# A two-layer hybrid decoder trunk: first x fetched already transposed, products by parts at the layer joins, smaller masks

## The reference, cut to what matters

```
for l in range(2):
    h = h + mixer_sublayer(h, ...)      # below
    h = h + ffn_sublayer(h, ...)        # rms_norm; silu(h@w_gate)*(h@w_up); @w_down; rms_norm

# mixer_sublayer
z = rms_norm(x, norm_pre) @ w_in        # c_q 384 | c_kv 256 | k_r 32 | conv 2*512 | pool 512 | gates 3*1024
y_attn = attention, 8 heads, causal, from rms_norm(c_q) @ w_uq, rms_norm(c_kv) @ w_uk, @ w_uv
y_conv = silu(layer_norm(conv31(a * sigmoid(g)))) @ w_conv_o
y_pool = (pooled differences @ pool_w per group of 128 * pool_scale) @ w_pool_o
out = rms_norm((g0*y_attn + g1*y_conv + g2*y_pool) @ w_mix_o, norm_post)
```

## Time and profile before

| | |
|---|---|
| median of three runs | 823.91 us (823.85 to 823.97) |
| profiled execution, its own time | 823.19 us |
| its span | 821.4 us |
| TensorE matmul busy | 801.1 us, 98% of the span |
| VectorE busy | 554.3 us, 67% |
| ScalarE busy | 428.5 us, 52% |
| GpSimd busy | 92.4 us, 11% |
| DMA | 144.44 MB, mean 176 GB/s |

### The profile page before, as it was taken

How to read it: one execution, slowest core, us unless ns; L and a number is a source line. 1 busy time by engine, 2 the same in 40 slices (tenths; PEclk the granted TensorE clock), 3 DMA queues, 4 the chain that set the end, 5 groups by cost and what they waited for, 6 DMA issues and landing times.

```text
span 821.4 us, 10272 instructions
## 1 busy us (share of the span) xinstructions
PE 801.1 (98%) x3924; PEld 675.4 (82%) x3924; DVE 554.3 (67%) x770; ACT 428.5 (52%) x607; POOL 92.4 (11%) x112
## 2 busy tenths in 40 slices
PE   5999999999999999999999999999999999999996
PEld 4898888878878888988879988888887888889885
DVE  5598898879565555554476988897886655555543
ACT  4668655653464444544374675556435544445431
POOL 3520000113220000000140100002304000000000
PEclk9999999999999999999999999999999999999999
DMA  8572644546466555555454544345564655555531
GB/s 302 189 231 78 232 153 138 163 141 219 134 197 233 186 198 186 179 181 185 147 178 156 205 178 156 128 154 164 169 202 153 232 182 184 189 188 172 189 128 52
DMA packets 41233, 144.44 MB, mean 176 GB/s; under 512 B 4704, under 2 KB 4960, under 8 KB 41184
## 3 DMA queue, kind: packets, MB, share of 16 engines
q1 hardware_dynamic: 40896, 142.34, 52.0%
q0 software_dynamic: 144, 0.92, 0.3%
q10 hardware_dynamic: 144, 0.52, 0.2%
HBM read 142.71 MB, written 1.05 MB: 175 GB/s over the span
## 4 chain that ended last, share of the span: by engine, by line
PE 92%; DVE 3%; ACT 1%; issue 1%; POOL 1%; DMA 1%; SPq 0%; DVEq 0%; ACTq 0%
PE acc L374 28%; PE acc L376 27%; PE acc L375 27%; PE tp L446 4%; PE misc L612 1%; DVE w_lo L1077 1%; PE misc L628 1%; POOL w_lo L1427 1%; ACT w_hi L760 1%; PE tp L461 1%; DMA pos_i<-pos 1%; DVE tp L1091 0%; PE misc L570 0%; DVE xT_lo L1098 0%; PE misc L607 0%
## 5 line engine op out<-in xcount | busy, mean ns | idle before, releaser
L1077 DVE TENSOR_TENSOR w_lo<-raw,w_hi 128x1024 fp32r<-128x1024 f32 (+2 forms) x243 | 302.4, 1250 | 163.5 <-ACT w_hi L760 161.2
L760 ACT ACTIVATE w_hi<-raw 128x1024 fp32r<-128x1024 f32 (+3 forms) x254 | 260.7, 1034 | 220.2 <-PE acc L376 208.8
L374 PE MATMUL acc<-w_hi,xT_hi 128*128 128x512 f32 (+3 forms) x800 | 308.3, 385 | 6.2 <-DVE xT_lo L1098 4.1
L376 PE MATMUL acc<-w_hi,xT_lo 128*128 128x512 f32 (+3 forms) x800 | 301.4, 377 | 0.0
L375 PE MATMUL acc<-w_lo,xT_hi 128*128 128x512 f32 (+3 forms) x800 | 300.9, 376 | 0.0
L374 PEld LDWEIGHTS acc<-w_hi,xT_hi 128*128 128x128 f32 x800 | 151.1, 189 | 35.0 <-DVE xT_lo L1098 3.7
L376 PEld LDWEIGHTS acc<-w_hi,xT_lo 128*128 128x128 f32 x800 | 150.8, 189 | 27.1
L375 PEld LDWEIGHTS acc<-w_lo,xT_hi 128*128 128x128 f32 x800 | 151.3, 189 | 24.4
L374 PE MATMUL acc<-w_hi,hT_hi 128*128 128x512 f32 (+1 forms) x300 | 118.1, 394 | 0.0
L376 PE MATMUL acc<-w_hi,hT_lo 128*128 128x512 f32 (+1 forms) x300 | 116.4, 388 | 0.0
L375 PE MATMUL acc<-w_lo,hT_hi 128*128 128x512 f32 (+1 forms) x300 | 116.3, 388 | 0.0
(11 more groups left out here) (127 smaller groups left out, 522.3 us busy)
## 6 DMA issues: line engine op xcount, KB each, us to landing
raw<-weights SPq DMA_DIRECT2D x248, 512.0 KB, 3.4
raw<-weights SPq DMA_DIRECT2D x14, 384.0 KB, 3.4
raw<-weights SPq DMA_DIRECT2D x8, 288.0 KB, 3.0
gain<-gains SPq DMA_DIRECT2D x4, 512.0 KB, 6.5
out_rows<-x_sb SPq DMA_DIRECT2D x4, 256.0 KB, 2.0
const<-consts POOLq DMA_DIRECT2D x1, 896.0 KB, 8.8
x_sb<-x_rows ACTq DMA_DIRECT2D x1, 512.0 KB, 5.0
x_sb<-x_rows SPq DMA_DIRECT2D x1, 512.0 KB, 4.8
```

The source lines that it names most:

```text
L374: pe.matmul(out, a_hi, b_hi, start=start, stop=False)
L376: return pe.matmul(out, a_lo, b_hi, start=False, stop=stop)
L760: ins = act.activation(w_hi[:, s, first:end], raw[:, s, first:end], ACT.Copy, scale=by)
L1077: ins = dve.tensor_tensor(w_lo[:, s, 0:width], raw[:, s, 0:width], f(w_hi[:, s, 0:width]), ALU.subtract)
```

## The change

The first layer's x is also given by the host in transposed form (`x_cols`, two tiles of 128 x 1032, with the first norm's gain in eight columns), and is fetched ahead of the weights; it is scaled, rounded and subtracted where it lies, so the first layer has no transposes of x. The rows of x come later, since only the norm's statistics and the residual need them. The constants are fetched by GpSimd after the first five units are rounded. Until data is there TensorE multiplies zeros, 16 float32 matmuls of 128 columns. In every `first_group` the three products of a unit are no longer together for each k but by part, and the waits for the low weight and the low x stand ahead of the part that needs them; in the first layer unit 4 moves out of the group. All five weight units of a start are lowered on VectorE in the first layer, and GpSimd keeps two of three at the other joins. In `entry` on ScalarE the fourth unit is rounded ahead of the squares of t = 1. The pool matrices leave the ring (135 units a layer) for a tile of their own, and their matmuls are done after gate unit 2. `norm_mean` is done after gate unit 22, and `conv_var` one unit and two gate products earlier on VectorE. The mask is written on the diagonal block alone, and the scores of t = 1 are made in two blocks of 128 columns for each head.

```diff
-POOL_LO = {(l, u) for l in range(LAYERS) for u in (U_FFN, U_FFN + 1, U_FFN + 3)}
-POOL_LO |= {(0, 1), (0, 3)} | {(l, u) for l in range(1, LAYERS) for u in (0, 1, 3)}
+POOL_LO = {(l, u) for l in range(LAYERS) for u in (U_FFN, U_FFN + 1)}
+POOL_LO |= {(l, u) for l in range(1, LAYERS) for u in (0, 1)}
+MT_AFTER, MEAN_AFTER = 2, 22
...
-            sp.dma_start(x[:, 0, :], x_d[0:P, :]).then_inc(x_in[0], 16)
-            sp.dma_start(const[:, 0:K_ONE], const_d[:, 0:K_ONE]).then_inc(const_in, 16)
-            sp.dma_start(par[:, :, :], par_d).then_inc(const_in, 16)
-            sp.dma_start(pos_i[:, :], pos_d).then_inc(const_in, 16)
+            def load_columns(t):
+                edges = (0 if t == 0 else KD, KD + 512, KD + D)
+                for h in range(2):
+                    c = slice(edges[h], edges[h + 1])
+                    sp.dma_start(x_cols[:, t, c], xc_d[t * P:(t + 1) * P, c]).then_inc(xc_in[t][h], 16)
+            load_columns(0)
...
                     load(l, u, unit_width(u))
+                    if l == 0 and u == U_G + 3:
+                        load_columns(1)
+                    if l == 0 and u == U_G + 4:
+                        for t in range(TOK):
+                            sp.dma_start(x[:, t, :], x_d[t * P:(t + 1) * P, :]).then_inc(x_in[t], 16)
+                    if u == U_POOL:
+                        load_pool_weights(l)
...
-            pe.wait_ge(const_in, 48)
+            pe.wait_ge(zeros_set, 1)
+            for _ in range(WARM):
+                pe.matmul(misc[:, 1, 0:P], diag[:, 0:P], diag[:, P:SEQ], start=True, stop=True)
...
-                        for i in range(5):
+                        for i in range(4 if given else 5):
...
                             elif i % 2 == 0:
-                                tp_emptied(pe, l, TPN[f"{name}{2 * t + i // 2}"])
+                                pe.wait_ge(tp_hi, hi0 + h)
                             if t == 0:
-                                unit_ready(u0 + i)
-                            mm = tok_mm(base + u0 + i, t, [2 * i % KD, 2 * i % KD + 1], 512,
-                                        [acc[:, 2 * (i // 4) + t, :]], XT, 0, KD - 1)
+                                pe.wait_ge(hi_done, base + u0 + i + 1)
+                            def low_x(last):
+                                if i < 4 and i % 2 == 0:
+                                    tp_emptied(pe, l, TPN[f"{name}{h}"])
+                                return products(xT_lo, w_hi, last)
+                            def low_w(last):
+                                if t == 0:
+                                    unit_ready(u0 + i)
+                                return products(xT_hi, w_lo, last)
...
+                            products(xT_hi, w_hi)
+                            if given and t == 0:
+                                low_x(False)
+                                mm = low_w(True)
+                            else:
+                                low_w(False)
+                                mm = low_x(True)
...
-                    pe.matmul(split3(misc[:, n % 2, 0:2 * keys], 2), ident_r[:, :],
-                              mask_r[:, SEQ - keys:SEQ].unsqueeze(1).to_broadcast((P, 2, keys)),
-                              start=True, stop=False)
+                    pe.matmul(split3(misc[:, n % 2, 0:2 * keys], 2)[:, :, keys - P:keys], ident_r[:, :],
+                              mask_r[:, :].unsqueeze(1).to_broadcast((P, 2, P)), start=True, stop=False)
...
+                        for k in range(t + 1):
+                            mm = pe.matmul(misc[:, n % 2, i * keys + k * P:i * keys + (k + 1) * P],
+                                           q_t[h // 4][0:QK, h % 4, tokens(t)],
+                                           k_t[h // 4][0:QK, h % 4, tokens(k)], start=False, stop=i == 1 and k == t)
...
+                    if i == MT_AFTER:
+                        pool_products()
+                    if i == MEAN_AFTER:
+                        norm_mean()
...
-                    his(u0, u0 + (3 if post else 1))
+                    his(u0, u0 + 3)
                     for h in range(2):
                         hi_scaled(f"{name}{h}", xT_hi[:, 4 * h:4 * h + 4, tokens(0)])
+                    his(u0 + 3, u0 + 4)
+                    wide_square(at, r_post + 1, 1, post)
+                    his(u0 + 4, u0 + 5)
...
 # VectorE
-                x_parts("X", 0, C_PRE, 0 if l == 0 else None)
-                los(1 if l == 0 else 0, 3)
+                x_parts("X", 0, C_PRE)
                 if l:
+                    los(0, 4)
                     post_norm(l - 1, 1, 1)
+                    los(4, 5)
+                    x_parts("X", 1, C_PRE)
+                else:
+                    los(0, 4)
+                    x_parts("X", 1, C_PRE)
+                    los(4, 5)
...
-                conv_centre()
-                los(54, 56)
+                los(53, 54)
+                conv_var()
+                los(54, 55)
                 gate_both(2, 0, "POOLO")
-                conv_var()
-                los(56, 57)
+                los(55, 56)
                 conv_scale()
...
-                los(70, 73)
+                los(69, 73)
                 post_norm(l, 1, 0)
-                los(73, 75)
+                los(73, 74)
                 x_parts("F", 1, C_PREF)
...
 # GpSimd
-            pool.wait_ge(const_in, 48)
...
                 if l == 0:
-                    lo(1)
-                    lo(3)
-                    pool.dma_start(const[:, K_ONE:NCONST], const_d[:, K_ONE:NCONST]).then_inc(late_in, 16)
+                    pool.wait_ge(hi_done, 5)
+                    pool.dma_start(const[:, 0:K_ONE], const_d[:, 0:K_ONE]).then_inc(const_in, 16)
+                    pool.dma_start(pos_i[:, :], pos_d).then_inc(pos_in, 16)
                     norm(R_X)
                     norm(R_X + 1)
+                    pool.dma_start(par[:, :, :], par_d).then_inc(par_in, 16)
+                    pool.dma_start(const[:, K_ONE:NCONST], const_d[:, K_ONE:NCONST]).then_inc(late_in, 16)
```

More of the change, by code:

```diff
@@ L206, in build @@
         hid = u_sb
+        x_cols = gates[:, :, 2 * D - KD:3 * D]
         cq = gates[:, :, D:D + Q_RANK + CKV_W]
@@ L323, in stat_ready, with given_x @@
             eng.wait_ge(r_done, l * NSTAT + n + 1)
+        def given_x(name):
+            t, h = divmod(int(name[1:]), 2)
+            return x_cols[:, t, KD + 512 * h:KD + 512 * (h + 1)]
         def rstd(l, n):
@@ L785, in hi_scaled @@
                     w = dst.shape[1] * dst.shape[2]
-                    act.activation(dst, split3(tp[:, TPN[name] % 2, 0:w], dst.shape[1]), ACT.Copy
-                                   ).then_inc(tp_hi, 1)
+                    src = given_x(name) if l == 0 and name[0] == "X" else tp[:, TPN[name] % 2, 0:w]
+                    act.activation(dst, split3(src, dst.shape[1]), ACT.Copy).then_inc(tp_hi, 1)
                 def hi_T(name, dst, by=1.0):
@@ L1449, in _ @@
                 if l == 0:
+                    pool.wait_ge(const_in, 16)
+                    pool.wait_ge(pos_in, 16)
                     angles()
@@ L1488, in _ @@
             norm(R_DOWN + 1, LAYERS - 1)
-def split_width(u):
-    return 2 if u == U_MT else unit_width(u)
 def unit_width(u):
@@ L1503, in unit_width @@
         return HEADS * QK
-    return 512 if u == U_MT else WU
+    return WU
 def weight_stream(a):
```

232 lines of the change are left out of this document (124 added, 108 removed), and 8 rows, old and new, of the table LAST_UNIT.

## The result

The changed kernel takes 811.44 us (median of four runs, 811.23 to 814.55), the kernel before 823.94 beside it: a ratio of 0.986, 95% interval 0.985 to 0.987. The run at 814.55 had a mean granted clock of 0.995, the other three 0.998 or 0.999. The forecast was 810.2, its range 807.8 to 814.0. The profiled execution took 811.29 with a span of 809.2, for 821.4 before, so 12.2 us of span went.

What follows compares the result with a forecast made beforehand. TensorE's own sequence bounds the kernel (matmuls 98% of the span). Gains 6.2 + 4.4 + 1.3 + 0.75 + 1.05 = 13.7 us off 823.19 give 809.5; the median, 0.7 above, is 810.2; range 807.8 to 814.0.

Steps and rivals of the forecast that it cites:

- The start: From the first transfers to unit 5: TensorE reaches unit 5 at 21.8 instead of 28.01, a gain of 6.2 us.
- The 742 KB less are 742 / 512 x 1.28 = 1.85 us, so unit 0 lands at about 5.95: At the start: fewer bytes ahead of weight unit 0, priced at 1.28 us per 512 KB, land it 1.85 us sooner.
- The prediction's lower bound: At the start: half-length x_cols rows take double time, losing 1.3 us; with the clock, a gain of 4.3.
- if unit 0 is rounded later than 6.5: Sign at the start: it would show that the order of the transfers did not pay as worked out.
- The start pays less: Rival: x late, or first products at 1.2 GHz again; start worth 4.3 to 5.4, time 811.0 to 812.1; chance 0.18.
- The zeros: Before the first product: they lift the clock, end between 4.5 and 8 us, and cost 0 to 0.3.
- The joins: MIX to F0 twice, DOWN to G once: two stalls and their refills go, 1.48 each, 4.4 us.
- the 0.7 us of cover: At the joins: new x is there at 230.2, its transposes come up at 230.9, despite VectorE's extra low part.
- Pool matrices: K's transposes no longer wait for VectorE's subtraction: 0.65 a layer, 1.3 us, bounds 0.5 and 1.7.
- Masks: Smaller mask for t = 1, less the cost of more score instructions: 0.75 us gained, from -0.6 to 0.9.
- Convolution's norm: TensorE's waits at the variance (0.19) and the spread (0.33) go: 0.52 a layer, 1.05 us.
- The slower rival: Constants on GpSimd's queue, sharing rings with the weights, land too late for the conv transposes; 828 if at 50; chance 0.02.

Runs made afterwards that it cites:

- experiment 8: The changed kernel with the old start (x by rows, transposes on TensorE, constants first, no zeros), the order by parts kept: 815.52 us.
- experiment 9: The changed kernel with x_cols of t = 0 in one transfer of whole rows instead of two of half rows: 809.98 us.
- experiment 1: The changed kernel without the sixteen matmuls of zeros: 813.00 us.
- experiment 6: The changed kernel with the scaling of the convolution's norm one low part earlier on VectorE: 810.36 us.
- experiment 10: The changed kernel with the two halves of x issued on ScalarE's queue, the weights alone on SP's: 812.94 us.
- experiment 7: The changed kernel with the edit of experiment 6, and MIX waiting for the second pair of transposed branches only at t = 1: 810.58 us.
- experiment 3: The changed kernel with the products unit by unit and token by token in the old order, not by parts: 813.87 us.
- experiment 4: The changed kernel with the fourth unit's low part on GpSimd again at the three later joins, the order by parts kept: 811.61 us.
- experiment 5: The changed kernel with the pool matrices' matmuls, roundings and subtractions before the gates again, their own tile kept: 813.24 us.
- experiment 2: The changed kernel with the mask on the whole row again and the scores of t = 1 in one piece for each head: 811.86 us.
- experiments 9 to 11: experiment 9, experiment 10, and the changed kernel with weight unit 0 alone on ScalarE's queue, x heading SP's: 810.56 us for this last.

## Why the prediction was right, point by point

**What bounds the kernel: right.** Every term was read from a distance between matmuls and each gain came out of such a distance; the page's busy time fell by only 2.2 us while the span fell by 12.2.

**The start: right mechanism, wrong size.** 4.87 us for 6.2, and 4.17 by experiment 8. The step that failed is "The 742 KB less are 742 / 512 x 1.28 = 1.85 us, so unit 0 lands at about 5.95". It went by bytes at the pace of the kernel before. Unit 0 was released at 6.80 and unit 3 at 11.17, 1.4 late, and from 4 to 7 us the engines moved 279 to 332 GB/s for the 406 to 418 of experiment 9. With x in one piece the step holds: unit 0 landed at 6.10 there and unit 5 came at 22.0, for 5.95 and 21.8. The prediction's lower bound had short rows in it (double time, 1.3 us) but took them as unlikely. Its reason was not the one that came, for x itself was on time; and its two terms, 1.3 and the 0.8 of the clock, make 4.1 and not the 4.3 given. The rest follows from the weights: the first product 1.0 late, unit 5 1.3 late. The sign "if unit 0 is rounded later than 6.5" came. The wait before t = 1, forecast at 0.8, was 14.81 - 14.06 - 0.23 = 0.52 (the row at 13.83 holds two products, the second 0.23 after the first). The gain of 4.87 and the median of 811.44 lie within what the rival "The start pays less" gave (4.3 to 5.4; 811.0 to 812.1). So it was this rival that came, by the transfers and not by the clock, and with the weights late rather than x, which was on time.

**The zeros: right for the changed kernel.** They end at 6.94, before unit 0 is rounded, so they cost nothing (0 to 0.3 was forecast), and by experiment 1 they give 0.75. In after the first products followed the zeros by 1.1 us and stood 0.53 / 2 apart. The rival's clock did come in two of the experiments: after a pause of 1.92 us (experiment 6) and of 2.57 (experiment 10) the products were 0.43 apart. After one of 2.33 (experiment 7) and one of 2.74 (experiment 3) they were at the upper level, so the length of the pause alone does not tell. In the two that fell the zeros had come to 0.11 us each at 6.0 and 6.2 us, in the two that stayed at 5.1 and 5.3; four traces are too few to say whether that is the reason. The Trainium skill's rule that idling brings the throttled clock back (TensorE: Matmul & The Clock Gate, part 1) agrees with the first two. The rival's price was right: "some eight of them cold, 8 x 0.2 = 1.6, of which 0.8 is hidden" leaves 0.8, and both experiment 1 beside after and experiment 6 beside 7 show 0.75.

**The joins: right,** 4.46 us for 4.4. Both stalls went with their refills, and the 0.7 us of cover sufficed: the transposes at 224.62 follow at once. The first stall was given to the low part's move to VectorE together with the order. Experiment 3 shows that the move is enough by itself, and experiment 4 that the order would have taken 0.58 of the 0.81 without it.

**Pool matrices: right,** 0.75 a layer for 0.65 (experiment 5 gives 0.73 and 0.75).

**Masks: right,** 0.73 in all by experiment 2 for 0.75. The mask's row is 0.28 long where products stand ahead of it and 0.36 behind the transposes (at 122.31 in after), so the sign "always 0.28" was too strict.

**Convolution's norm: too small,** 0.74 a layer for 0.52. The stalls of 0.19 and 0.33 went, and a slow refill of 0.1 behind each too: 171.74 to 172.21 before is 0.47, and 165.55 to 165.91 after 0.36; 175.39 to 175.73 before is 0.34, and 168.76 to 169.00 after 0.24. The prediction counted such refills at the joins and behind the pool matrices, and forgot them here.

**What was missing: the wait at MIX,** +0.94. By the convolution's norm PE stands 6.7 us earlier than before and VectorE's scale only 5.5, with a low part right ahead of it. All that was said of what is late next was "needed some 2 us later", an estimate for the low parts and gates right behind `conv_var`; the end of VectorE's list, at the merges, was not followed. Experiment 6 settles it.

**The sum.** Errors of -1.3 (start), +0.4 (norm), +0.2 (pool), +0.1 (joins) and -0.9 (MIX) make -1.5, and the span fell by 12.2 us for the 13.7 of the sum; the median missed by 1.2. That it came so near is in part luck: two stages gave more than forecast and hid a part of what the start and MIX lacked. The slower rival was nowhere: constants by GpSimd's queue delay nothing (experiment 8). They don't share a ring with the weights either, as the rival had it: the page has them on a queue of their own (q0, 256 packets). What stays open is why two short-row transfers at the head of a queue slow single packets of the weights behind them on it; experiments 9 to 11 show that they do, not by what mechanism. Open too is why the release of unit 0 differs between kernels with the same start (6.67 to 8.01 us in the traces of experiments 2 and 6), where the edit stands far behind it. With x in one piece the four runs of experiment 9 lie within 0.34 us.

## What to carry to other kernels

When TensorE is nearly full, read the distances between starts and price each stall with its refill (about 0.1 us here), wherever it stands. When an edit moves the bounding engine forward, follow the other engines' lists to the end of the stage and ask which item now has the least room: here one 1.2 us operation ahead of the one that mattered cost 0.47 us a layer, far from the edit. Where two edits aim at one stall, try each without the other: here each took most or all of it alone. When two traces are compared, line them up at the event that decides: from the first product to unit 5 the kernel without zeros takes only 0.27 us more than after, from the release of unit 3 it takes 0.79, and 0.75 is what it loses. And at a kernel's start don't price the first transfers by bytes alone: splitting the first one to have half of it sooner got it 1.2 us sooner, and everything behind it later.

## What the runs showed of the hardware that was not expected

- With two transfers with 2 KB rows at the head of the queue and the weights behind them on it, the rate was 279 to 332 GB/s from 4 to 7 us (769 to 991 KB in eight traces). With one transfer with 4 KB rows it was 406 to 418 (1,242 and 1,155 KB in two), and the kernel was 1.46 us faster by medians. The short rows took 0.08 to 0.09 us each; slow were 7 to 14 packets of the weights behind them, over 0.5 us each for the usual 0.16.
- Products on zeros lift the clock as real ones do, but it can fall again behind them: it did where a pause of 1.92 or 2.57 us followed (granted 0.50), and did not in two others with 2.33 and 2.74. Eight products at 0.43 us then cost 0.75 us at unit 5 of the 1.6 that they take more.
- After a stall TensorE's next product takes 0.31 to 0.34 us to the following one, where 0.23 is usual, so a stall costs about 0.1 more than its wait.
